# GpSimd makes the low parts of the 60 early input tiles of each expert layer, VectorE before

## The reference, cut to what matters

```python
def block(xb):                                                 # xb: tokens x 1024
    q = (xb @ w_q).reshape(n, 8, 2, 128)                        # 8 heads, two halves
    s = einsum('nhpc,pkc->nhpk', q, subkeys)                    # 128 keys for each half
    sv, si = top_k(s, 16)
    cand = sv[:, :, 0, :, None] + sv[:, :, 1, None, :]          # 16 x 16 sums
    cand_id = si[:, :, 0, :, None] * 128 + si[:, :, 1, None, :]
    fv, fi = top_k(cand.reshape(n, 8, 256), 16)
    eid = take_along_axis(cand_id.reshape(n, 8, 256), fi)       # 16 experts of 16384
    act = gelu(einsum('nhkd,nd->nhk', u_tab[eid], xb))
    return einsum('nhk,nhkd->nd', softmax(fv) * act, v_tab[eid])
```

## Time and profile before

| | us |
|---|---|
| median of 3 executions | 3491.95 (3485.2 to 3493.96) |
| profiled execution | 3497.0, its span 3495.3 |
| PE busy in the span | 3239.5 (93%) |
| DVE busy | 2078.9 (59%) |
| ACT busy | 1234.2 (35%) |
| POOL busy | 111.7 (3%) |
| low parts on DVE by L2056, both expert layers | 512 instructions, 627.9 us |

### The profile page before, as it was taken

How to read it: one execution, slowest core, us unless ns; L and a number is a source line. 1 busy time by engine, 2 the same in 40 slices (tenths; PEclk the granted TensorE clock), 3 DMA queues, 4 the chain that set the end, 5 groups by cost and what they waited for, 6 DMA issues and landing times.

```text
span 3495.3 us, 52926 instructions
## 1 busy us (share of the span) xinstructions
PE 3239.5 (93%) x20456; PEld 2780.3 (80%) x20456; DVE 2078.9 (59%) x3709; ACT 1234.2 (35%) x1842; POOL 111.7 (3%) x135
## 2 busy tenths in 40 slices
PE   6998998999988999688899999999889899999998
PEld 2566996996767979478899999887668799999986
DVE  2453554554345550439996666685438997666686
ACT  1132433432124431122454444433322354444433
POOL 0100000000000000003100000000002200000000
PEclk8999998999999999699999999999889999999999
DMA  7403554555213534024466665674224466665674
GB/s 274 170 1 118 184 186 170 185 186 197 87 37 132 184 135 152 2 97 142 166 226 228 209 219 205 224 240 145 93 70 146 143 228 245 204 217 211 205 245 138
DMA packets 190525, 580.71 MB, mean 166 GB/s; under 512 B 16768, under 2 KB 61824, under 8 KB 185504
## 3 DMA queue, kind: packets, MB, share of 16 engines
q1 hardware_dynamic: 185120, 541.04, 44.8%
q10 hardware_dynamic: 4608, 33.56, 2.3%
q0 software_dynamic: 640, 4.00, 0.3%
HBM read 543.92 MB, written 34.60 MB: 166 GB/s over the span
## 4 chain that ended last, share of the span: by engine, by line
PE 84%; DVE 11%; ACT 3%; DMA 1%; issue 1%; DVEq 0%; ACTq 0%; SPq 0%; POOL 0%; POOLq 0%
PE ps L926 29%; PE ps L967 25%; PE ps L917 4%; PE ps L803 4%; PE ps L761 4%; PE ps L1168 3%; PE ps L898 2%; PE ps L870 2%; PE ps L806 2%; PE ps L886 2%; DVE w_split L2056 1%; PE ps L955 1%; PE ps L949 1%; DVE arena L1670 1%; PE ps L1133 1%; DVE arena L2079 1%
## 5 line engine op out<-in xcount | busy, mean ns | idle before, releaser
L926 PE MATMUL ps<-x_split,w_split 128*128 128x256 f32 x9312 | 1188.2, 286 | 71.6 <-DVE w_split L2056 41.1
L926 PEld LDWEIGHTS ps<-x_split,w_split 128*128 128x128 f32 x9312 | 1163.1, 193 | 96.6 <-issue 75.7
L967 PE MATMUL ps<-w_split,h_split 128*128 128x512 f32 x3864 | 915.7, 391 | 2.5 <-DVE w_split L2056 2.5
L967 PEld LDWEIGHTS ps<-w_split,h_split 128*128 128x128 f32 x3864 | 713.8, 188 | 143.8 <-issue 2.9
L2056 DVE TENSOR_TENSOR w_split<-ring,w_split 128x1024 fp32r<-128x1024 f32 x512 | 627.9, 1227 | 324.7 <-ACT w_split L1517 323.8
L1517 ACT ACTIVATE w_split<-ring 128x1024 fp32r<-128x1024 f32 x512 | 541.2, 1058 | 387.3 <-PE ps L967 350.8
L1868 DVE TENSOR_TENSOR w_split<-ring,w_split 128x1024 fp32r<-128x1024 f32 x198 | 242.3, 1226 | 237.0 <-ACT w_split L1482 237.0
L1482 ACT ACTIVATE w_split<-ring 128x1024 fp32r<-128x1024 f32 x198 | 209.0, 1059 | 329.6 <-PE ps L926 226.6
L1525 ACT ACTIVATE arena<-ps 128x256 f32<-128x256 f32 (+1 forms) x256 | 98.6, 385 | 460.3 <-PE ps L926 460.3
L917 PE MATMUL ps<-arena,ring 128*128 128x256 f32 (+1 forms) x672 | 152.6, 391 | 9.3 <-DVEq L1664 7.1
L803 PE MATMUL ps<-arena,ring 128*128 128x512 f32 (+1 forms) x416 | 154.1, 525 | 4.8 <-ACTq L1274 4.8
(11 more groups left out here) (262 smaller groups left out, 2555.2 us busy)
## 6 DMA issues: line engine op xcount, KB each, us to landing
ring<-in_peer_u SPq DMA_DIRECT2D x256, 512.0 KB, 3.3
ring<-in_peer_v SPq DMA_DIRECT2D x256, 512.0 KB, 4.2
ring<-in_ffn_in SPq DMA_DIRECT2D x132, 512.0 KB, 3.2
ring<-in_ada SPq DMA_DIRECT2D x96, 512.0 KB, 4.5
ring<-in_ffn_out SPq DMA_DIRECT2D x66, 512.0 KB, 3.2
spread_rows<-arena ACTq DMA_DIRECT2D x32, 1024.0 KB, 4.1
arena<-spread_rows SPq DMA_DIRECT2D x20, 1536.0 KB, 8.4
ring<-in_pq SPq DMA_DIRECT2D x32, 512.0 KB, 3.2
```

The source lines that it names most:

```text
L926: last = mm(dst, w_split[:, w, wp, at:at + P], rhs[rp], start=(first and i == 0), stop=(final and i == 2), skip_group_check=shared)
L967: last = mm(ps[:, 2 * r + c, :], h_split[:, ph, hp, r * P:(r + 1) * P], w_split[:, b[3], wp, c * 512:(c + 1) * 512], start=(first and i == ...
```

## The change: the low parts of u = 0 to 59 move from DVE to POOL

`early_low` now stands in POOL's function `choose` and writes the same tiles with the same subtraction, counted by a semaphore of its own, `weights_low_by_gpsimd`. PE's `go_in(u)` waits on that one for u below 60. The counts of `weights_low` that the other tiles wait for are lowered by the 60 of each layer. DVE's 60 calls are gone. In the changed kernel the lines are shifted: L662 is the new low part on POOL, L941 is `passes`, L2112 the cast that ends `best_of`, L2163 to L2167 are the operands of the spread.

```diff
@@ -415,7 +415,7 @@
         sum_ready = sem("sum_ready")
         res_ready, ln_mean, ln_centred, ln_squared, ln_var, ln_scaled, ln_x, x_high = (sem(n) for n in (
             "res_ready", "ln_mean", "ln_centred", "ln_squared", "ln_var", "ln_scaled", "ln_x", "x_high"))
-        w_high, w_low = sem("weights_high"), sem("weights_low")
+        w_high, w_low, w_low_g = sem("weights_high"), sem("weights_low"), sem("weights_low_by_gpsimd")
         gate_ready, hid_made, hid_high, hid_ready = (sem(n) for n in ("gate_ready", "hid_made", "hid_high", "hid_ready"))
         lam_sum, lam_exp = sem("lam_sum"), sem("lam_exp")
         pool_out = sem("pool_mixed")
@@ -653,11 +653,26 @@
                             last = t_(rows, rows, over(best_key_f[:, 2 * h + i, t, :], TOPK), ALU.mult)
                     last.then_inc(k_product, 1)
 
+                first, w_base = first_block(f"hidden{l}"), split_before(f"hidden{l}")
+
+                def early_low(u):
+                    at = first + (2 * u + 1 if u < QUERIES else u + QUERIES)
+                    w, slot = at % SPLIT, at % R
+                    pool.wait_ge(w_high, w_base + u + 1)
+                    t_(w_split[:, w, 1, :], ring[:, slot, :], w_split[:, w, 0, :].bitcast(F32), ALU.subtract)\
+                        .then_inc(w_low_g, 1)
+
+                early_low(0)
+                early_low(1)
                 for h in range(PH):
                     sums(h)
+                    early_low(2 * h + 2)
                     if h:
                         products(h - 1)
+                    early_low(2 * h + 3)
                 products(PH - 1)
+                for u in range(2 * PH + 2, AHEAD):
+                    early_low(u)
                 pool.drain().then_inc(stage["g"], 1)
 
             for l in (2, 3):
@@ -1146,7 +1161,10 @@
                 def go_in(u, bank, blk, split):
                     if not isinstance(u, int) or u >= 2:
                         pe.wait_ge(gelu_made, u + (KEYS * lb - 1))
-                    pe.wait_ge(w_low, split)
+                    if isinstance(u, int) and u < AHEAD:
+                        pe.wait_ge(w_low_g, AHEAD * lb + u + 1)
+                    else:
+                        pe.wait_ge(w_low, split - AHEAD * (lb + 1))
                     for k in range(KD):
                         last = passes(ps[:, 4 + bank, 0:T], blk[3], k * P, [x_split[:, i, k, :] for i in range(2)],
                                       k == 0, k == KD - 1)
@@ -1154,7 +1172,7 @@
 
                 def go_out(j, ph, blk, opens=False, final=False):
                     pe.wait_ge(coef_ready, j + (KEYS * lb + 1))
-                    pe.wait_ge(w_low, blk[2] + (w_base - first - QUERIES + 1))
+                    pe.wait_ge(w_low, blk[2] + (w_base - first - QUERIES - AHEAD * (lb + 1) + 1))
                     token_rows(ph, blk, opens, final)
 
                 def spread(s):
@@ -2056,17 +2074,12 @@
                     v.tensor_tensor(w_split[:, w, 1, :], ring[:, slot, :], w_split[:, w, 0, :].bitcast(F32),
                                     ALU.subtract).then_inc(w_low, 1)
 
-                def early_low(u):
-                    place.at = first + (2 * u + 1 if u < QUERIES else u + QUERIES)
-                    place.steps(dve, 1, 1, lambda _, par, b: low(b[0], w_base + u + 1))
-
-                def top16(batch, low_between):
+                def top16(batch):
 
                     for wait, values, _, scores, _ in batch:
                         wait()
                         last = v.max(values[:, 0:8], scores)
                     chain(last)
-                    low_between()
                     for _, values, _, scores, left in batch:
                         v.match_replace(left, values[:, 0:8], scores, NEG)
                     for _, values, indices, scores, _ in batch:
@@ -2094,7 +2107,7 @@
                     if h:
                         batch += [(summed(h - 1), top[:, h - 1, t], top_at[:, h - 1, t], cand[:, (h - 1) % 2, t, :],
                                    rest_sums[:, t, :]) for t in range(2)]
-                    top16(batch, lambda: early_low(2 * h + 2))
+                    top16(batch)
                     if h < PH:
                         v.tensor_copy(best_key_f[:, 2 * h:2 * h + 2], best_key[:, 2 * h:2 * h + 2]).then_inc(k_best, 1)
 
@@ -2119,11 +2132,8 @@
                                                picked[:, 4 * (h % 2) + 2 * i:4 * (h % 2) + 2 * i + 2], AX_X, ALU.add)
                     return last
 
-                early_low(0)
-                early_low(1)
                 for h in range(PH + 1):
                     best_of(h)
-                    early_low(2 * h + 3)
                     if h:
                         finals(h - 1)
                     if 2 <= h < PH:
@@ -2133,7 +2143,6 @@
                 v.tensor_tensor(by_head, top, top[:, :, :, 0:1].to_broadcast([P, PH, 2, TOPK]), ALU.subtract)\
                     .then_inc(k_shift, 1)
                 key_of(PH - 2)
-                early_low(QUERIES + 4)
                 dve.wait_ge(k_exp, l - 1)
                 w = top_w.rearrange("p t (h k) -> p t h k", h=PH)
                 chain(v.tensor_reduce(top_sum, w, AX_X, ALU.add))
@@ -2143,11 +2152,8 @@
                 key_of(PH - 1).then_inc(k_pick, 1)
                 v.tensor_copy(key_row, const("iota"))
                 v.tensor_copy(places, const("iota").unsqueeze(2).to_broadcast([P, KEYS, GROUP]))
-                early_low(QUERIES + 5)
-                early_low(QUERIES + 6)
                 dve.wait_ge(k_keep, 2 * (l - 1))
                 tables()
-                early_low(QUERIES + 7)
 
                 def hot(s):
                     b, at = s % 2, slice(s * GROUP, (s + 1) * GROUP)
@@ -2164,9 +2170,6 @@
 
                 for s in range(U_SPREAD):
                     hot(s)
-                    early_low(QUERIES + U_PICK + s)
-                for u in range(QUERIES + U_PICK + U_SPREAD, AHEAD):
-                    early_low(u)
 
                 def weighed(j, blk, lag):
 
```

## The result

The changed kernel takes 3721.14 us (median of four, 3720.24 to 3723.23) against 3492.95 (four, 3485.2 to 3498.5): a ratio of 1.065, 95% interval 1.0635 to 1.0668. The forecast was 3696, and the measured time lies inside its range of 3628 to 3785. The profiled execution took 3723.2, its span 3721.5, which is 226.2 more than the 3495.3 of before.

The account below looks back on a forecast made before the run. PE was taken to bound the spread, with idle time only in selection and tail. Per layer 56 + 7.6 + 7 + 31 = 102, two layers 204, on 3497.0 gives 3701, less 5: 3696 us; range 3628 to 3785 (8 in 10).

Parts of the forecast that it names:

- The chain in selection: Selection: the low part queues behind sums that wait for best_of, so TensorE idles 9 us; round 24.45 instead of 15.09, +56.
- best_of to the cast: Selection round: from the end of the scores to the cast that ends best_of, 8.7 us.
- low part: Selection round: the low part of tile 2h+2 on GpSimd, behind the sums, takes 2.2 us (1.7 to 2.9).
- TensorE's own work: Selection round: go_in to scores, query, go_in and scores at full clock, 10.3 us.
- restart: Selection round: TensorE runs slow after its idle gap, 1.8 us a gap (1.3 to 2.4).
- the second low part of a round is covered: Selection: low part of 2h+3 ends 6.8 us after the first, before TensorE comes to it at 9.7, so costs nothing.
- The first round: Selection, head 0 to head 1: best_of is shorter without candidates, so the chain adds less, +7.6 us.
- Tail: Selection's end to first spread: low parts wait behind products(7), picks turned at 37 instead of 29.5 us; +7.
- The spread: Spread steps: VectorE's two-input operands and GpSimd's low part exclude each other, 5.56 instead of 4.54 us a step; +31 a layer.
- The free spread: Rival 1: selection chain holds but the spread costs nothing; 3634 us, chance 0.15.
- The longer chain: Rival 2: low part 2.9 us, first go_in of a round at half speed, 3.0 more; about 3780 us, chance 0.16.
- The third: Rival 3: low parts come in time in selection, TensorE's 13.5 us bounds a round, not slower; 3456 us, chance 0.02.

Follow-up runs that it names:

- the second: Against the changed kernel, GpSimd makes only the low parts of tiles 24 to 59 (spread), VectorE those of 0 to 23: 3568.84 us, ratio 1.0213.
- sixth: Changed kernel, but from tile 24 on GpSimd fills the low part with zeros instead of reading two tiles and subtracting: 3642.04 us, ratio 1.0422.
- seventh experiment: Changed kernel, but from tile 24 on GpSimd writes the low part by two one-input copies of the weight tile: 3678.52 us, ratio 1.0526.
- the third experiment: Changed kernel, but both low parts of a selection round stand ahead of the sums on GpSimd: 3561.04 us, ratio 1.0188.

## Why the prediction was right, step by step

A layer was forecast at +102 us (56 + 7.6 + 7 + 31) and measured at +113.0 (62.1 + 7.1 + 9.5 + 34.2). No large miss of one term was hidden by another.

**The chain in selection.** Right. TensorE waits for the first L662 behind the sums, 9.51 us, where 9 was forecast. Its terms, predicted and measured: best_of to the cast 8.7 and 8.8 (1628.74 to 1637.51); sums 1.35 and 1.22; low part 2.2 and 2.75; TensorE's own work 10.3; restart 1.8 and about 2.1 (the three input products above take 4.9 in the mean against 3.1, the scores behind them up to 0.4 more). The round is 25.4, not 24.45. The size that was off is the low part's, and twice over: alone it is 2.37, and at this place it first waits for an equality of VectorE. The order of VectorE's instructions had shown that neighbour; I had written of the exclusion only in the spread. The aside that the second low part of a round is covered holds: it ended 5.8 us after the first, and TensorE came to it 9.6 us after the first. (Its own terms give 5.0 and 8.6, not the 6.8 and 9.7 written there.)

**The first round.** +7.6 was forecast. From the scores of head 0 to those of head 1 it took 20.6 us instead of 13.55, +7.1.

**Tail.** +7 forecast, +9.5 measured. The first part went as I had it: the picks were turned 36.3 us after the last scores, where I had 37, and what they waited for is TensorE's own queue, the three input products behind the low part of 18. Rows of the changed kernel's TensorE:

```profile
1756.29 10.36 PE L941 MATMUL ps<-x_split,w_split 128*128 128x256 f32 x72 [4.31 <-POOL w_split L662]
1766.48 1.50 PE L1194 MATMUL ps<-consts,arena 128*128 128x128 f32 x12
...
1782.05 2.78 PE L1186 MATMUL ps<-res,arena 128*128 128x128 bf16 x24 [5.44 <-DVE arena L2167]
```

The step that was off comes after it. Three rows of VectorE:

```profile
1763.08 0.42 DVE L2148 TENSOR_REDUCE arena<-arena 128x16 f32<-128x256 f32 x1 [10.69 <-ACT arena L1582]
...
1773.20 2.42 DVE L2214 CAST x<-res 128x256 bf16<-128x256 f32 x1
1775.66 2.48 DVE L2216 TENSOR_TENSOR res<-res,x 128x256 f32<-128x256 f32 x1
```

Two instructions of the tables, 0.29 and 0.42 us alone, took 2.4 and 2.5 beside low parts of GpSimd, 4.2 us more, where I had allowed for at most one such meeting and one us. From the first cast of the tables to the first spread VectorE needed 9.97 us instead of 6.92. So the +9.5 are 6.8 to the turned picks, -0.4 to the tables and 3.05 behind them. VectorE's own path to the picks was not the last one, as forecast, but ahead by only 1 us (its last instruction for them ended at 1765.43), since it waited 10.69 us for ScalarE's exponentials (L1582), which stand in ScalarE's queue behind the activation of tile 18, and so behind that low part.

**The spread.** Right in cause and nearly in size: 5.61 a step against 5.56, 34.2 a layer against 31. The 2 us that the first steps were to hide did not show, and the last product took 1.1 longer. The fills and the copies show the cause: with GpSimd as long occupied but reading nothing the step is 4.43, with two copies that read one input each 5.04, with the low part and its two inputs 5.61. The Trainium skill's rule (SBUF — State Buffer, section Who interferes with whom), which names exactly this pair of instructions and excepts a GpSimd instruction that only writes, agrees with all three, and with bf16 operands too, for which the trace before had no row. One sentence of mine was not quite right: VectorE's work did cost something in the spread before, the 0.11 us between 4.54 and 4.43. VectorE's four instructions fill 4.54 exactly, and TensorE's busy time, in which ends overlap, had hidden the difference.

**The rivals.** The free spread is refuted by the second, sixth and seventh experiment. The longer chain was right in direction only (its terms add up to 3772, not 3780): the low part in a round came near its 2.9 with 2.75, but the restart of about 2.1 did not reach 3.0. The third, that the low parts come in time, described what happens when the order is changed: its 13.5 us round is that of the third experiment (13.55).

## What to carry to other kernels

When work moves to an idle engine, look first at what stands ahead of it in that engine's queue and what that waits for. Here a wait on the very step that the next tile was to run beside cost 69 us a layer, and two lines in another order turned it into a gain of 9. Then compare which instructions run at the same time: GpSimd reading SBUF beside VectorE with two inputs from SBUF made the durations add up here; beside maxima, index searches and reductions a low part or a product cost nothing.

## What the runs showed of the hardware that was not expected

- GpSimd's low part (128x1024 fp32, two inputs) takes 2.33 us at least, twice VectorE's 1.21; a fill of that size takes 0.96, and a copy holds VectorE off for 0.84.
- VectorE's casts were held off as well, though they read one input: one of 0.29 us took 2.42 beside a low part (2.37 with the spread's alone on GpSimd).
- A gap of TensorE of 6.3 us and one of 9.5 cost much the same, 1.6 to 2.4 and 1.3 to 2.4 us in the input product behind it; with matmuls in the gap the cost is gone.
